# Value sums of two expert layers: plain fp32 for half of tile 1, wider gathered rows for tile 0, value table by chunk

## What is computed

```python
act = jax.nn.gelu(jnp.einsum('thkd,td->thk', peer_u[eb], xb), approximate=False) * gb
return jnp.einsum('thk,thkd->td', act, peer_v[eb])
```

## Time and profile before

| | |
|---|---|
| time before, median of 3 runs | 2210.45 us (2208.16 to 2211.26) |
| the profiled execution's own time | 2205.84 us |
| its span | 2204.0 us |
| PE / PEld busy | 1981.9 us (90%) / 1824.2 us (83%) |
| DVE / ACT / POOL busy | 1500.1 us (68%) / 1041.7 us (47%) / 859.5 us (39%) |
| mean granted TensorE clock | 0.969 |
| DMA | 594.70 MB, mean 270 GB/s |

### The profile page before, as it was taken

How to read it: one execution, slowest core, us unless ns; L and a number is a source line. 1 busy time by engine, 2 the same in 40 slices (tenths; PEclk the granted TensorE clock), 3 DMA queues, 4 the chain that set the end, 5 groups by cost and what they waited for, 6 DMA issues and landing times.

```text
span 2204.0 us, 34958 instructions
## 1 busy us (share of the span) xinstructions
PE 1981.9 (90%) x13778; PEld 1824.2 (83%) x13778; DVE 1500.1 (68%) x2783; ACT 1041.7 (47%) x2013; POOL 859.5 (39%) x626
## 2 busy tenths in 40 slices
PE   6999999867998899999998899877998888899998
PEld 6999988766997899888886789877898887788886
DVE  5644331468887965888887243376588798699887
ACT  5455442123234666555555462122233558666556
POOL 0000000368677323676630000076566734345640
PEclk9999999988999999999999999998999999999999
DMA  5433444899999777899983435699999963799985
GB/s 214 153 120 130 163 167 152 317 374 400 386 397 409 242 228 254 293 319 315 336 268 122 172 116 172 230 401 399 392 368 388 380 212 123 245 314 321 307 297 194
DMA packets 150641, 594.70 MB, mean 270 GB/s; under 512 B 19255, under 2 KB 20919, under 8 KB 134734
## 3 DMA queue, kind: packets, MB, share of 16 engines
q1 hardware_dynamic: 97230, 407.89, 52.0%
q0 software_dynamic: 53248, 184.58, 22.5%
HBM read 591.35 MB, written 1.05 MB: 269 GB/s over the span
## 4 chain that ended last, share of the span: by engine, by line
PE 59%; DMA 18%; issue 10%; DVE 8%; ACT 4%; POOL 1%; SPq 0%; DVEq 0%; ACTq 0%; POOLq 0%
PE bank L959 13%; PE bank L998 11%; DMA ut_sb<-in_ut_dram 9%; PE bank_n L998 7%; PE bank L922 4%; DMA nt_sb<-in_vl_dram,idx_sb 4%; PE bank L575 3%; PE bank L576 3%; PE bank L577 3%; PE bank L978 3%; DMA big_sb<-in_u_dram,idx_sb 2%; DMA junk_sb<-in_vl_dram,idx_sb 2%; PE bank L835 2%; PE bank L670 1%; PE bank L855 1%
## 5 line engine op out<-in xcount | busy, mean ns | idle before, releaser
L959 PE MATMUL bank<-nt_sb,ut_sb 128*128 128x128 f32 x4096 | 511.5, 282 | 57.5 <-DMA ut_sb<-in_ut_dram 53.1
L959 PEld LDWEIGHTS bank<-nt_sb,ut_sb 128*128 128x128 f32 x4096 | 486.4, 196 | 73.7 <-DMA ut_sb<-in_ut_dram 50.2
L2265 POOL DMA_INDIRECT big_sb<-in_u_dram,idx_sb x256 | 268.7, 1050 | 250.4 <-ACT big_sb L1110 148.6
L2265 POOL DMA_INDIRECT nt_sb<-in_vl_dram,idx_sb x172 | 248.2, 1443 | 270.3 <-DVE x_sb L1616 137.3
L1110 ACT ACTIVATE big_sb<-bank 128x512 f32<-128x512 f32 (+13 forms) x292 | 134.1, 471 | 416.1 <-PE bank L959 195.5
L2229 POOL TENSOR_TENSOR sm_sb<-sm_sb,vec_sb 128x1 f32<-128x1 f32 (+2 forms) x24 | 19.5, 814 | 730.5 <-DVE sm_sb L1613 725.0
L2036 DVE CUSTOM_DVE_ANT_0 big_sb<-big_sb,bank_n 128x1024 f32<-128x1024 f32 x170 | 205.4, 1211 | 95.3 <-DMA big_sb<-in_u_dram,idx_sb 92.1
L1110 ACT ACTIVATE v_hi<-nt_sb 128x1024 fp32r<-128x1024 f32 x162 | 172.7, 1066 | 147.9 <-PE bank L998 67.1
L2286 POOL TENSOR_TENSOR big_sb<-big_sb,nt_sb 128x1024 f32<-128x1024 f32 x86 | 206.3, 2400 | 3.2 <-DMA big_sb<-in_u_dram,idx_sb 1.6
L1610 DVE TENSOR_TENSOR v_lo<-nt_sb,v_hi 128x1024 fp32r<-128x1024 f32 x162 | 198.0, 1222 | 0.0
L575 PE MATMUL bank<-n_hi,w_hi 128*128 128x256 f32 x608 | 181.7, 299 | 16.0 <-DVE w_lo L1610 10.3
(11 more groups left out here) (249 smaller groups left out, 4152.2 us busy)
## 6 DMA issues: line engine op xcount, KB each, us to landing
ut_sb<-in_ut_dram SPq DMA_DIRECT2D x256, 512.0 KB
big_sb<-in_wall_dram SPq DMA_DIRECT2D x122, 1024.0 KB, 5.3
nt_sb<-in_v_dram SPq DMA_DIRECT2D x154, 512.0 KB
sw_sb<-in_v_dram SPq DMA_DIRECT2D x102, 512.0 KB
big_sb<-in_u_dram,idx_sb POOLq DMA_INDIRECT x256
nt_sb<-in_vl_dram,idx_sb POOLq DMA_INDIRECT x172
sw_sb<-in_v_dram SPq DMA_DIRECT2D x8, 320.0 KB
nt_sb<-in_v_dram SPq DMA_DIRECT2D x8, 320.0 KB
```

The source lines that it names most:

```text
L959: i = e.matmul(hs(bk, c % 4), UT[:, c % DR, k * 128:(k + 1) * 128], TN[1][:, k, :], start=k == 0, stop=k == 7)
L2265: return e.indirect_dma_start(out, None, table, bass.IndirectOffsetOnAxis(ap=IDX[:, k:k + 1], axis=0))
```

## The change

Four things are changed together.

1. FD goes from 384 to 640: tile 0's first 640 columns come from gathered rows (2560 bytes each instead of 1536), and the product makes only its last 384, as one matmul per part. The three gather buffers are 640 wide; two of them move into the constants tile (CST), over constants that are not used later. There is one accumulator, `X[:, 0, 0:640]`, in place of two: each addition waits for the one before, and LSUM and its final addition are gone.
2. Tile 1's first 512 columns (RAW_COLS) are multiplied unsplit: one plain fp32 matmul, `GM[:, 1, c, :]` times the raw chunk, as the first instruction of PE's step. It waits only for the chunk's load (and in step 0 for GM). Tile 1's last 512 columns stay split, one matmul per part.
3. So ACT and DVE split only columns 512 to 1023 in steps with tile 1, and only 640 to 1023 in the steps of tile 0 alone. SP's load of a slot waits in addition for the plain matmul that read it.
4. The value table is laid out by chunk (`transpose(1, 0, 2)`): the 128 rows of a chunk lie one behind the other, 512 KB in one piece.

```diff
--- before.py
+++ after.py
@@ -13,8 +13,8 @@
 D = 1024
 WR = 4
 UR = 8
-FD = 384
-VD = D - FD
+FD = 640
+RAW_COLS = 512
 DR = 4
 TAIL = 8
 POOLDOT = 3
@@ -301,10 +301,9 @@
         VSL = [SW[:, 0:D], SW[:, D:2 * D]] + [NT[:, o:o + D] for o in (3072, 1024, 2048)]
         vslot = lambda s: s % 5
         HB = [NT[:, o:o + 512].rearrange("p (c t) -> p c t", c=4) for o in (1024, 1536, 3072, 3584)]
-        LSL = [NT[:, 0:FD], NT[:, FD:2 * FD], JUNK[:, :].bitcast(F32)[:, 0:FD]]
-        LSUM = SUB[:, :, :].rearrange("p a b -> p (a b)")[:, 0:FD]
+        LSL = [NT[:, 0:FD], CST[:, C_US * 128:C_US * 128 + FD], CST[:, C_US * 128 + FD:C_US * 128 + 2 * FD]]
         sums = [[banks[0], banks[1]], [banks[4], banks[5]]]
-        MM = (((FD, 704), (704, D)), ((0, 512), (512, D)))
+        total = [sums[0][0][:, 0:D - FD], [sums[1][0][:, :], sums[1][1][:, :]]]
         UP = {(1, 0): 30, (1, 1): 32, (2, 0): 74, (2, 1): 76}
         SQUARE = {1: 34, 2: 78, "co": 42}
         PQ = {1: 46, 2: 82}
...
@@ -547,8 +546,10 @@
                         e.wait_ge(*(dense_v.at("w", l, 31) if s < 4 else dense_p.at("c", l, 127)))
                     else:
                         e.wait_ge(*val_v.at("vl", l, s - 5))
+                        if 1 in STEPS[s - 5][1]:
+                            e.wait_ge(*val_p.at("whole", l, s - 5))
                     lo_ = FD if ts == (0,) else 0
-                    e.dma_start(VSL[vslot(s)][:, lo_:D], table[:, c, lo_:D]).then_inc(*v_in[vslot(s)].up(l, s))
+                    e.dma_start(VSL[vslot(s)][:, lo_:D], table[c, :, lo_:D]).then_inc(*v_in[vslot(s)].up(l, s))
 
             def store():
                 for t in range(2):
@@ -987,6 +988,15 @@
                         yield T_VAL[l][0]
                         for x in range(2):
                             take(ring_b, ("sums", l, x), (fin_v, "fin", l, 1, 1))
+                    if 1 in ts:
+                        yield T_VAL[l][0] + T_VAL[l][1] * s - 0.5
+                        e.wait_ge(*v_in[vslot(s)].at(l, s))
+                        if s == 0:
+                            e.wait_ge(*gate_a.at("gm", l, 1, 31))
+                            e.wait_ge(*gate_v.at("gm", l, 1, 31))
+                            e.wait_ge(*dense_v.at("w", l, 31))
+                        i = e.matmul(total[1][0], GM[:, 1, c, :], VSL[vslot(s)][:, 0:RAW_COLS], start=s == 0, stop=s == LAST[1])
+                        i.then_inc(*val_p.up("whole", l, s))
                     for part, (x, y) in enumerate(((gh, VH), (gl, VH), (gh, VL))):
                         yield T_VAL[l][0] + T_VAL[l][1] * s + 0.6 * part
                         if part == 0:
@@ -994,9 +1004,8 @@
                         else:
                             e.wait_ge(*val_v.at(("", "gl", "vl")[part], l, s))
                         for w, t in enumerate(ts):
-                            for m, (n0, n1) in enumerate(MM[t]):
-                                i = e.matmul(sums[t][m][:, 0:n1 - n0], x[:, w, :], y[:, b, n0:n1],
-                                             start=part == 0 and s == 0, stop=part == 2 and s == LAST[t])
+                            i = e.matmul(total[1][1] if t else total[0], x[:, w, :], y[:, b, RAW_COLS if t else FD:D],
+                                         start=part == 0 and s == 0, stop=part == 2 and s == LAST[t])
                         if part:
                             i.then_inc(*val_p.up(f"p{part}", l, s))
 
@@ -1493,7 +1502,7 @@
 
             def values(l):
                 for s, (c, ts) in enumerate(STEPS):
-                    b, n = s % 2, len(ts)
+                    b, n, low = s % 2, len(ts), RAW_COLS if 1 in ts else FD
                     yield T_VAL[l][0] + T_VAL[l][1] * s - (5 if s < 3 else 2)
                     e.wait_ge(*v_in[vslot(s)].at(l, s))
                     if s > 1:
@@ -1501,7 +1510,7 @@
                         e.wait_ge(*val_v.at("vl", l, s - 2))
                     elif s == 0:
                         e.wait_ge(*dense_p.at("c", l, 127))
-                    copy(VH[:, b, :], VSL[vslot(s)]).then_inc(*val_a.up("vh", l, s))
+                    copy(VH[:, b, low:D], VSL[vslot(s)][:, low:D]).then_inc(*val_a.up("vh", l, s))
                     yield T_VAL[l][0] + T_VAL[l][1] * s - (1 if s else 0.5)
                     if s == 0:
                         e.wait_ge(*dense_v.at("w", l, 31))
...
@@ -2091,37 +2100,31 @@
             def lows(l):
                 for n in range(128):
                     yield low_beat(l, n) + 6
-                    dst = X[:, 0, 0:FD] if n % 2 == 0 else LSUM
-                    if n == 1:
-                        e.wait_ge(*sel_p.at("s", l, 1, 3))
-                    if n > 1:
-                        e.wait_ge(*low_v.at(l, n - 2))
+                    dst = X[:, 0, 0:FD]
+                    if n:
+                        e.wait_ge(*low_v.at(l, n - 1))
                     e.wait_ge(*low_in[n % 3].at(l, n))
-                    if n == 1:
-                        ts(dst, LSL[n % 3], H[:, n:n + 1], ALU.mult).then_inc(*low_v.up(l, n))
-                    else:
-                        stt(dst, LSL[n % 3], H[:, n:n + 1], dst, ALU.mult, ALU.add).then_inc(*low_v.up(l, n))
-                yield low_beat(l, 128) + 6
-                e.wait_ge(*low_v.now())
-                tt(X[:, 0, 0:FD], X[:, 0, 0:FD], LSUM, ALU.add).then_inc(*low_v.up("sum", l))
+                    stt(dst, LSL[n % 3], H[:, n:n + 1], dst, ALU.mult, ALU.add).then_inc(*low_v.up(l, n))
 
             def values(l):
                 for s, (c, ts_) in enumerate(STEPS):
-                    b, n = s % 2, len(ts_)
+                    b, n, low = s % 2, len(ts_), RAW_COLS if 1 in ts_ else FD
                     yield T_VAL[l][0] + T_VAL[l][1] * s - 0.4
                     gs = GM[:, ts_[0]:ts_[-1] + 1, c, :]
                     gh, gl = [x[:, b, 0:n * 128].rearrange("p (a t) -> p a t", a=n) for x in (GH, GL)]
                     e.wait_ge(*val_a.at("gh", l, s))
                     tt(gl, gs, f32(gh), ALU.subtract).then_inc(*val_v.up("gl", l, s))
                     yield T_VAL[l][0] + T_VAL[l][1] * s
-                    tt(VL[:, b, :], VSL[vslot(s)], f32(VH[:, b, :]), ALU.subtract).then_inc(*val_v.up("vl", l, s))
+                    tt(VL[:, b, low:D], VSL[vslot(s)][:, low:D], f32(VH[:, b, low:D]), ALU.subtract).then_inc(*val_v.up("vl", l, s))
 
             def sums_out(l, t):
-                for m, (n0, n1) in enumerate(MM[t]):
+                for m, (n0, n1) in enumerate(((0, RAW_COLS), (RAW_COLS, D)) if t else ((FD, D),)):
                     yield T_VAL[l][0] + T_VAL[l][1] * LAST[t] + 3.2 + 0.5 * m
+                    if t == 0:
+                        e.wait_ge(*low_v.now())
                     e.wait_ge(*val_p.at("p2", l, LAST[t]))
                     xs = X[:, t, n0:n1]
-                    tt(xs, xs, sums[t][m][:, 0:n1 - n0], ALU.add).then_inc(*fin_v.up("fin", l, t, m))
+                    tt(xs, xs, total[1][m] if t else total[0], ALU.add).then_inc(*fin_v.up("fin", l, t, m))
 
             def norm_2():
                 yield 965
@@ -2391,8 +2394,8 @@
         "subk2": np.concatenate([f("peer_k1_2")[0].T, f("peer_k2_2")[0].T], axis=1),
         "sguw": f("sgu_w_2")[0].transpose(2, 0, 1).reshape(128, 512),
         "sgub": f("sgu_b_2")[0].reshape(1, 512),
-        "u1": f("peer_u")[0], "ut1": chunked(f("peer_u")[0]), "vl1": f("peer_v")[0][:, :FD], "v1": f("peer_v")[0].reshape(128, 128, D),
+        "u1": f("peer_u")[0], "ut1": chunked(f("peer_u")[0]), "vl1": f("peer_v")[0][:, :FD], "v1": f("peer_v")[0].reshape(128, 128, D).transpose(1, 0, 2),
     }
     return {k: np.ascontiguousarray(v) for k, v in out.items()}
```

More of the change, by code:

```diff
@@ L494, in rows @@
                 yield 960
-                e.wait_ge(*val_v.at("gl", 1, STEPS.index((127, (0, 1)))))
+                e.wait_ge(*val_p.at("p1", 1, STEPS.index((127, (0, 1)))))
                 e.dma_start(LNR[0:1, :], a["rows"][R_LN:R_LN + 1, :]).then_inc(*row_in.up("ln", 1))
@@ L501, in rows @@
                 yield 1077
-                e.wait_ge(*low_v.at("sum", 1))
+                e.wait_ge(*sel_p.at("s", 1, 1, 3))
                 e.dma_start(SUB[:, 0, :], a["subk2"]).then_inc(*subk2_in.up("all"))
@@ L1516, in final @@
                 b = T_VAL[l][0] + T_VAL[l][1] * LAST[t] + 4.5
-                yield from squares(("fin", l, t), X[:, t, :], (b, b + 0.4), [([] if t else [low_v.at("sum", l)]) + [fin_v.at("fin", l, t, 0)], [fin_v.at("fin", l, t, 1)]])
+                yield from squares(("fin", l, t), X[:, t, :], (b, b + 0.4), [[fin_v.at("fin", l, 1, 0) if t else low_v.at(l, 127)], [fin_v.at("fin", l, t, t)]])
             def norm_2():
@@ L2393, in lay_out @@
         "sgub": f("sgu_b_2")[0].reshape(1, 512),
-        "u1": f("peer_u")[0], "ut1": chunked(f("peer_u")[0]), "vl1": f("peer_v")[0][:, :FD], "v1": f("peer_v")[0].reshape(128, 128, D),
-        "u2": f("peer_u_2")[0], "ut2": chunked(f("peer_u_2")[0]), "vl2": f("peer_v_2")[0][:, :FD], "v2": f("peer_v_2")[0].reshape(128, 128, D),
```

(2 more changed lines are left out.)

## The result

The changed kernel takes **2238.49 us** (median of 4, 2238.15 to 2238.97) against 2210.86 (4 runs) of the kernel before: a ratio of 1.0123 [1.0106, 1.0141] (in brackets the 95% interval), slower. Forecast was 2184 with a whole range of 2148 to 2228; the measured time lies 10 us above its upper end. The profiled execution took 2238.15 us, its span is 2236.4, at a mean granted clock of 0.97.

A forecast was written before the change was run, and what follows sets the result against it. PE was taken to pace layer 2, with layer 1 slightly above it through its gather chain. Savings of 1 + 9 + 6.5 + 8 + 5 less 3 lost made 26.5 us less: 2184 us, range 2148 to 2228.

The forecast's parts named there:

- PE: Value steps with both tiles: PE's step becomes 2.08 us against 2.28, 0.20 less.
- DVE, and the single tiles: Value steps: v_lo 0.69 us, additions 0.87; tile 0 alone 0.9 a step, 8 us saved; tile 1 alone 5 saved.
- Layout: Value table laid out by chunk instead of rows 512 KB apart: taken as 0 us.
- The gates: Layer 2's gates: wider additions load DVE by between 0 and 5.2 us, 3 us lost taken.
- Ahead of layer 1's stage: Layer 1's gates: wider additions hidden by PE's full stretch, no cost; 5 us without that cover.
- POOL: POOL's part of a layer 1 gather, 1.69 us, falls by 0.5 with vl at 0.69.
- The gather's latency: Value steps: layer 2's middle latency 4.6 us, round 2.02, pace 2.19; layer 1 6.1 + 0.32 - 0.5, pace 2.40.
- the hand-over: Gather ring in the value steps: addition and hand-over together rise from 0.88 to 1.14 us.
- Layer 1's starting point: Layer 1 before the change: a buffer's round of 7.02 us over three buffers, 2.34 a step, pace 2.41.
- The slow rival: The gather ring replaces PE as pace in both layers, 2.52 and 2.47 us a step: 2226 us, chance 0.20.
- The upper bound of the layer 2 round: Layer 2's value steps: (5.96 + 0.64 + 1.14) / 3 = 2.58 us a step at most.
- a floor of 2.08 us for the DMA engines: Value steps: 0.852 MB a step at 409 GB/s takes 2.08 us, the same as PE's new floor.

The follow-up runs named there:

- b_rows640: The kernel before with gathers fetching 640 columns, of which additions use 384, buffers placed as in the changed kernel: 2242.67 us, ratio 1.0131 to the kernel before.
- a_rows384: The changed kernel with gathers fetching only 384 columns, additions still 640 wide: 2186.82 us, ratio 0.9891 to the kernel before.
- a_half_v: The changed kernel loading only columns 512 to 1023 of each chunk, gathers untouched: 2146.58 us, ratio 0.9712 to the kernel before.
- b_ring4: The kernel before with a fourth gather buffer of 384 columns: 2198.77 us, ratio 0.9931 to the kernel before.
- a_ring4: The changed kernel with a fourth gather buffer of 640 columns: 2157.11 us, ratio 0.9758 to the kernel before.

## Why the prediction was wrong

**PE: right.** The timeline of PE in the changed kernel, from the start of one step to the start of the next, with nothing late:

```profile
2169.91 1.02 PE L998 MATMUL bank<-nt_sb,big_sb 128*128 128x512 f32 x2
2170.36 0.74 PE L1007 MATMUL bank_n<-v_hi,g_hi 128*128 128x384 f32 x1
...
2171.99 1.02 PE L998 MATMUL bank<-nt_sb,big_sb 128*128 128x512 f32 x2
```

2171.99 - 2169.91 = 2.08 us, as summed from the earlier trace rows, against 2.28 before.

**DVE, and the single tiles: right.** The timeline of DVE holds an addition at 0.88 (0.87 forecast), v_lo at 0.69, and the steps of tile 0 alone:

```profile
2177.91 0.88 DVE L1625 SCALAR_TENSOR_TENSOR x_sb<-cst_sb,h_sb,x_sb 128x640 f32<-128x640 f32 x1
...
2179.04 0.69 DVE L1619 TENSOR_TENSOR v_lo<-sw_sb,v_hi 128x512 fp32r<-128x512 f32 x1
...
2208.49 0.55 DVE L1619 TENSOR_TENSOR v_lo<-sw_sb,v_hi 128x384 fp32r<-128x384 f32 x1
...
2213.41 0.55 DVE L1619 TENSOR_TENSOR v_lo<-nt_sb,v_hi 128x384 fp32r<-128x384 f32 x1
...
2215.94 0.69 DVE L1619 TENSOR_TENSOR v_lo<-nt_sb,v_hi 128x512 fp32r<-128x512 f32 x1
...
2227.26 0.69 DVE L1619 TENSOR_TENSOR v_lo<-sw_sb,v_hi 128x512 fp32r<-128x512 f32 x1
```

Six steps of tile 0 alone take 4.92 us, 0.82 each (0.9 forecast, 1.42 before); seven of tile 1 alone 11.3 (10.9 forecast, 13.2 before).

**Layout: right**, nothing. **The gates:** the part between the two value stages, the gates of layer 2 with it, grew by 1.8 us where 3 was summed; over the 14 traces it lasts 694 to 702 us whatever the change, so neither number can be told from nothing. Ahead of layer 1's stage 5.4 us appeared that were costed at nothing, with PE's full stretch named as the cover and 5 us as the price without it. PE is still full there (49.98 of 50). The first v_lo starts at 874.4 to 881.1 us in the four kernels with 384-column gathers and at 876.8 to 883.3 in the ten with wider ones: the two overlap, and whether the change costs anything there stays open.

**POOL: right.** Its part of a gather in layer 1 fell by 0.5, as forecast beside the halved vl:

```profile
1061.05 1.15 POOL L2268 DMA_INDIRECT nt_sb<-in_vl_dram,idx_sb  x1 [1.46 <-DVE x_sb L1625]
```

That is 1.69 beside a 1.22 us vl, 1.15 beside a 0.69 one. The gathers' width does not matter for it: the median is 1.69 in `b_rows640` and 1.15 in `a_rows384`.

**The gather's latency: this step failed.** The forecast took 4.6 us for layer 2, the middle between an idle stage and the longest that would have stayed hidden, which put the round below PE's floor, and added what layer 1 had stood above its own bound. No row of the trace stood behind it. The landing took 6.4, and the round (6.4 + 1.15) / 3 = 2.52 set the pace, 2.56 measured; the hand-over of 1.14 was right (1946.60 less 1945.44 is 1.16). In layer 1, 6.1 + 0.32 - 0.5 = 5.9 was taken and 6.5 measured: with POOL's part gone, the transfer itself grew from about 4.3 to 5.4 us. The 0.32 for the wider rows was their own bytes at full rate. What the runs show in its place is a price beside the chunk loads: wider rows alone took the landing in layer 2 to 6.1 us (`b_rows640`), and halving the loads beside them took it from 6.4 to 4.7 (`a_half_v`). That the rows queue with the chunk loads is the reading that fits both; the queue itself is not seen.

Layer 1's starting point was also less of a ring than the prediction had it. Its 2.34 is one round of the chain. The median landing of 6.0 gives (6.0 + 0.88) / 3 = 2.29, PE's pace, and a fourth buffer took 0.09 us of the 0.17 that the steps stood above 2.28 (`b_ring4`).

By stage, the forecast had -11 us for layer 1's value stage and -18 for layer 2's; measured +10 and +15. Those 21 and 33 us, with the 5.4 ahead of layer 1, less 1 between, are the 59 by which the profiled execution missed its 2179.

The slow rival had the mechanism and nearly the paces: 2.52 and 2.47 against 2.56 in both windows. Its 2226 is 12 us short. It got 0.20 because layer 2 showed no wait on a gather. But no wait at 2.28 us a step only says that three steps less the use are longer than the latency; it says nothing once the pace is to fall while the load grows. The upper bound of the layer 2 round, 2.58, was in the text, and the measured pace is at it: here, where the change took the slack that the latency lived on, the upper bound was the nearer row.

The prediction also let 0.852 MB a step at 409 GB/s stand as a floor of 2.08 us for the DMA engines. `a_ring4` reaches it with 403 GB/s, but PE's own floor is the same 2.08 and PE is full there, so no run shows that the DMA engines could not go faster. The Trainium skill's bound of about 358 GB/s for a core (DMA: Bandwidth & Descriptors, section Bandwidth) is exceeded over 100 us in that run; the same section has 425 GB/s measured on a core whose neighbour is idle, and this kernel runs on one core.

## What to carry to other kernels

A ring of gather buffers that sets the pace does so at (latency + use + hand-over) / buffers; take the latency from under the load that the changed kernel will have, not from a stage with slack. If that comes near the other engines' floor, add a buffer before widening the transfers: here the same change costs 0.6% to 1.2% with three buffers, and with four it takes 2157 us, 2.4% less than the kernel before, and is the fastest version that leaves nothing out. Against the kernel before with four buffers it is 1.9% less. The DMA engines' busy share was 0.96 in the slow case and 1.02 in the fast one, and told nothing of which it was; the rate, and who waits for whom, did.

## What the hardware showed unexpectedly

The latency of a gather in layer 2 rose from 4.2 to 5.0 us (three kernels) to 6.1 when the gathers alone were widened, 0.13 MB on a step's 0.72 (`b_rows640`). In the changed kernel it is 6.4, and it stayed at 6.6 when the rate went up from 332 to 403 GB/s with a fourth buffer. The busy share does not measure bytes: in the DMA views of 1950 to 2050 us q0's packets take 39.5% for 12.52 MB in the changed kernel and 39.8% for 15.48 MB in `a_ring4`, so a packet of the same size took a fifth less time where more was moved. That its time holds some waiting is the likely reading; it is not shown. In the changed kernel:

```profile
q0 software_dynamic: 3069, 12.52, 39.5%
```

and in `a_ring4`:

```profile
q0 software_dynamic: 3780, 15.48, 39.8%
```

Layer 1 keeps its mean step at about 2.3 us even with four buffers (2.33) or half the loads (2.30), though PE's floor is 2.08 there too. Its median step is 2.10 in both: ten or eleven steps of over 3 us make up nearly all the rest. In each of the two the four longest (4.3 to 5.8 us) begin 3 to 10 us after one of four 1 MB loads of other weights (`in_wall_dram`), which stand among layer 1's value steps and not among layer 2's. One of them in `a_half_v`, by the timelines of SP and DVE:

```profile
1009.09 0.50 SPq L361 DMA_DIRECT2D big_sb<-in_wall_dram  x1
...
1015.97 0.88 DVE L1625 SCALAR_TENSOR_TENSOR x_sb<-cst_sb,h_sb,x_sb 128x640 f32<-128x640 f32 x1 [3.01 <-DMA cst_sb<-in_vl_dram,idx_sb]
```

That these loads hold up the gathers and chunks is a reading of their order; no run leaves them out.
